# Two-layer decoder trunk on 8 cores: the first rows and mixer units issued one behind the other, norm rows and fourth feed-forward slot later, background casts placed anew

## What is computed

```python
h = layer_norm(DEEPNORM_ALPHA * h + mix, ln1_g[i], ln1_b[i])
h = layer_norm(DEEPNORM_ALPHA * h + sqrelu_mlp(h, mlp_w_up[i], mlp_w_down[i]), ln2_g[i], ln2_b[i])
gate = jax.nn.sigmoid(h @ ple_w_gate[i] + ple_b_gate[i])
h = h + gate * (p[i] @ ple_w_proj[i])
```

## Time and profile before

| | us |
|---|---|
| median of 3 runs | 3253.4 |
| the three runs | 3247.75, 3253.4, 3253.92 |
| the profiled execution, its own time | 3248.94 |
| its span, first to last instruction, slowest core (core 5) | 3247.1 |
| spans of the 8 cores | 3213.3 to 3247.1 |
| PE busy on core 5 | 3081.9 (95%) |
| PE idle on core 5 | 165.2 |

### The profile page before, as it was taken

The page is one execution under the profiler, slowest core; times in us unless marked ns, Lnnn a source line. Parts: engine busy times, 40 slices in busy tenths (PEclk is TensorE's granted clock), DMA queues, the critical chain, the costliest instruction groups (busy, mean ns, idle before and its releaser), DMA issues.

```text
span 3247.1 us, 46641 instructions; the slowest of 8 cores (3213.3 to 3247.1 us)
## 1 busy us (share of the span) xinstructions
PE 3081.9 (95%) x15776; PEld 1446.8 (45%) x15776; DVE 1475.4 (45%) x2583; ACT 1658.3 (51%) x2936; POOL 881.8 (27%) x551
## 2 busy tenths in 40 slices
PE   5989986899999999999999999999999999999998
PEld 2444443444444444444444444444444444444443
DVE  3460163625354555446443354556424455445614
ACT  3476044654556455544555545555564645655452
POOL 0240051314133242424213142232312224142402
PEclk9999998999999999999999999999999999999999
DMA  8749959578986465563635544463644644344441
GB/s 201 166 109 180 173 166 216 171 169 199 258 208 210 152 195 184 161 228 143 221 126 192 205 143 166 143 185 111 207 177 148 199 152 178 130 147 158 143 172 65
DMA packets 84760, 556.65 MB, mean 171 GB/s; under 512 B 9680, under 2 KB 9936, under 8 KB 27600
## 3 DMA queue, kind: packets, MB, share of 16 engines
q1 hardware_dynamic: 74304, 485.31, 42.7%
q0 software_dynamic: 10224, 68.36, 14.8%
HBM read 564.83 MB, written 85.46 MB: 200 GB/s over the span
## 4 chain that ended last, share of the span: by engine, by line
PE 82%; DMA 7%; DVE 6%; issue 3%; ACT 2%; SPq 0%; DVEq 0%; ACTq 0%; POOLq 0%
PE ps L725 31%; PE ps L1134 24%; PE ps L732 13%; PE ps L1167 6%; DMA mring<-ws 3%; PE ps L1067 2%; DMA xT<-xs 1%; PE ps L1176 1%; PE ps L763 1%; PE ps L1047 1%; DVE ar L751 1%; DVE h L787 1%; DMA h<-x 1%; DMA sring<-wsb 1%; PE ps L1027 1%
## 5 line engine op out<-in xcount | busy, mean ns | idle before, releaser
L725 PE MATMUL ps<-xT,mring 128*128 128x512 bf16 x4096 | 916.3, 381 | 14.2 <-DVE xT L773 5.7
L1134 PE MATMUL ps<-mring,ar 128*128 128x512 bf16 x4096 | 922.2, 379 | 5.2 <-DMA mring<-ws 3.1
L725 PEld LDWEIGHTS ps<-xT,mring 128*128 128x128 bf16 x4096 | 393.7, 98 | 491.3 <-issue 45.2
L1134 PEld LDWEIGHTS ps<-mring,ar 128*128 128x128 bf16 x4096 | 392.6, 98 | 466.9 <-issue 21.5
L781 POOL TENSOR_TENSOR h<-h,lnr_sb 128x1024 f32<-128x1024 f32 x128 | 306.9, 2401 | 853.2 <-ACT rstd L745 432.4
L732 PE MATMUL ps<-sring,xT 128*128 128x512 bf16 x2048 | 469.0, 386 | 6.7 <-DMA sring<-wsb 5.8
L1119 ACT ACTIVATE tmpa<-ps 128x512 f32<-128x512 f32 x512 | 304.7, 596 | 268.6 <-PE ps L725 266.5
L787 DVE SCALAR_TENSOR_TENSOR h<-h,ps 128x512 f32<-128x512 f32 x256 | 173.8, 681 | 566.5 <-PE ps L1134 512.5
L732 PEld LDWEIGHTS ps<-sring,xT 128*128 128x128 bf16 x2048 | 202.0, 100 | 255.7 <-issue 31.1
L782 POOL TENSOR_TENSOR h<-h,lnr_sb 128x1024 f32<-128x1024 f32 x128 | 305.0, 2389 | 12.7 <-POOL h L781 0.4
L1120 ACT ACTIVATE ar<-tmpa 128x512 bf16<-128x512 f32 x456 | 287.2, 630 | 40.8 <-ACT tmpa L1119 1.5
(11 more groups left out here) (139 smaller groups left out, 2750.5 us busy)
## 6 DMA issues: line engine op xcount, KB each, us to landing
mring<-wsb SPq DMA_DIRECT2D x224, 1024.0 KB, 5.7
sring<-wsb SPq DMA_DIRECT2D x116, 1024.0 KB, 6.1
lnr_sb<-lnr SPq DMA_DIRECT2D x32, 1024.0 KB, 5.9
wsb<-ws POOLq DMA_DIRECT2D x23, 1024.0 KB, 17.5
h<-x SPq DMA_DIRECT2D x32, 512.0 KB, 9.1
mring<-ws POOLq DMA_DIRECT2D x16, 1024.0 KB, 20.8
wsb<-mring SPq DMA_DIRECT2D x16, 1024.0 KB, 20.2
y<-h SPq DMA_DIRECT2D x32, 512.0 KB, 6.3
```

Of the source, the lines that this page charges most:

```text
L725: ins = h.matmul(ps[b.i][:], lhsT=wt[:, (m * 8 + kc) * 128:(m * 8 + kc + 1) * 128], rhs=xT[c][:, kc, :], start=(kc == 0), stop=(kc == 7))
L1134: ins = h.matmul(ps[b.i][:], lhsT=hid(kk)[:, t * 128:(t + 1) * 128], rhs=wt[:, kc * 512:(kc + 1) * 512], start=(kk == 0), stop=(kk == 31))
```

## The change

Five edits, all in the streams that issue DMAs.

1. The first three mixer casts used to be issued at once. Now cast 0 waits for the landing of row tile 1 of group 0, and casts 1 and 2 wait for the landing of cast 0.
2. The rows of group 1 waited for the first mixer cast; now they wait for row tile 3 of group 0.
3. The first load of the norm rows was issued first of all; now it waits for the landing of `sring` load 7 (second output-projection unit).
4. `mring` load 3, the fourth slot, had no wait of its own and was issued by POOL right behind the first three mixer casts (the row at 5.54 us below); now it waits for `sring` load 7, as load 2 did and does.
5. The 23 background casts have new places: before `mring` 4, 6, 8, 10, 12, 14, `sring` 9, 11, 13, 15, 17, `mring` 24 to 29 and 40 to 45; now `mring` 4, 6, 8, 10, 12, 14, 15, `sring` 19, 21, 23, `mring` 23, 25, 27, 29, 31 and 34, 36, ... 48.

```diff
--- before.py
+++ after.py
@@ -595,6 +595,7 @@
         cast_done = set()
 
         loads = {"mring": [], "sring": []}
+        first_rows = []
         bg = [L0_N + i for k in ("q", "up", "gt") for i in range(L1_UNITS[k], L1_UNITS[k] + {"q": 5, "up": 16, "gt": 2}[k])]
 
         def loader(R):
@@ -604,8 +605,8 @@
                 buf, res = R.slot(k)
                 uid = u + (L0_N if layer else 0)
                 also = []
-                if R is RM and k < 3:
-                    at = (2, 6, 7)[k]
+                if R is RM and k < 4:
+                    at = (2, 6, 7, 7)[k]
                     yield Until(lambda at=at: len(loads["sring"]) > at)
                     also = [loads["sring"][at]]
                 if uid in bg:
@@ -613,6 +614,9 @@
                     yield Until(lambda uid=uid: f"wsb{uid}" in S.last_w)
                 if uid not in cast_done:
                     cast_done.add(uid)
+                    if R is RS and k < 3:
+                        yield Until(lambda k=k: len(first_rows) > (1, 7, 7)[k])
+                        also = [first_rows[1]] if k == 0 else [mine[0]]
                     o = O("pool", lambda h, buf=buf, uid=uid: h.dma_start(out=buf[:], in_=ws_d[uid]), [], [res], CAST, dma_key="c" + res, also=also)
                     mine.append(o)
                     yield o
@@ -625,7 +629,7 @@
                     R.loaded = k + 1
 
         def caster():
-            places = [("mring", k) for k in range(4, 16, 2)] + [("sring", k) for k in (9, 11, 13, 15, 17)] + [("mring", k) for k in list(range(24, 30)) + list(range(40, 46))]
+            places = [("mring", k) for k in (4, 6, 8, 10, 12, 14, 15)] + [("sring", k) for k in (19, 21, 23)] + [("mring", k) for k in list(range(23, 32, 2)) + list(range(34, 49, 2))]
             todo = [(at, i, f"wsb{uid}", wsb_d[uid], ws_d[uid]) for i, (uid, at) in enumerate(zip(bg, places))]
             for j in range(2, NJ):
                 g, layer = job_of(j)
@@ -642,6 +646,7 @@
 
         def lnr_loader():
             yield Until(lambda: len(loads["sring"]) > 7)
+            first = loads["sring"][7:8]
             for i, e in enumerate(lnseq):
                 yield Until(lambda i=i: state["lnr_used"] >= i)
                 if e < 0 and -1 not in lnseq[:i]:
@@ -651,7 +656,7 @@
                 elif e < 0:
                     yield O("sp", lambda h: h.dma_start(out=lnr[:, 0, :], in_=bos_d[:, :]), ["bos"], ["lnr"], 5e5, dma_key="lnr")
                 else:
-                    yield O("sp", lambda h, e=e: h.dma_start(out=lnr[:].rearrange("p a d -> p (a d)"), in_=lnr_d[e]), [], ["lnr"], 1e6, dma_key="lnr")
+                    yield O("sp", lambda h, e=e: h.dma_start(out=lnr[:].rearrange("p a d -> p (a d)"), in_=lnr_d[e]), [], ["lnr"], 1e6, dma_key="lnr", also=first if i == 0 else ())
                 state["lnr"] = i + 1
 
         def p_loader():
@@ -699,12 +704,16 @@
         def load_h(c, g, layer=0):
             late = ()
             if layer == 0 and g >= 1:
-                at = 0 if g == 1 else first_unit[(g, 0)] + 4
-                yield Until(lambda: len(loads["sring"]) > at)
-                late = loads["sring"][at:at + 1]
+                at = first_unit[(g, 0)] + 4
+                if g > 1:
+                    yield Until(lambda: len(loads["sring"]) > at)
+                late = loads["sring"][at:at + 1] if g > 1 else first_rows[3:4]
             src = hs_d if layer else x_d
             for t in range(NT):
-                yield O("sp", lambda h, t=t: h.dma_start(out=h_tok[c][:, t, :], in_=src[g * G + t * 128:g * G + (t + 1) * 128, :]), [f"hs{g}_{t}"] if layer else [], hn(c, t), 5e5, dma_key=f"h{c}_{t}", also=late)
+                o = O("sp", lambda h, t=t: h.dma_start(out=h_tok[c][:, t, :], in_=src[g * G + t * 128:g * G + (t + 1) * 128, :]), [f"hs{g}_{t}"] if layer else [], hn(c, t), 5e5, dma_key=f"h{c}_{t}", also=late)
+                if len(first_rows) < 8:
+                    first_rows.append(o)
+                yield o
             h_named.add((g, layer))
 
         def spill(c, g):
```

## The result

| | before | after |
|---|---|---|
| median of 6 runs, us | 3251.56 | 3237.09 |
| ratio after to before, 95% interval | | 0.9962 (0.995 to 0.9973) |
| span of the slowest core in the profiled execution, us | 3247.1 | 3234.7 |
| mean span of the 8 cores, us | 3228.8 | 3220.8 |

Faster by 12 us by the ratio and 14 by the medians, where 25 were forecast; the time lies in the range, 11 us above the number.

A forecast was written before the change was run, and what follows sets the result against it. PE, busy 95% of the span, was taken as the bound, plus its 165 us of idle time. Gains 22 + 3 + 5 - 5 = 25 us off 3248.9 gave 3224, stated as 3226; range 3206 to 3246.

The forecast's parts named there:

- edits 1 to 4, to A: Start to the first up matmul: it comes at about 165.5 us, before at 187.44; a gain of 22, bounds 12 and 28.
- 5 (a): Stretch from 225 to 445 us: a background cast moved from its front gains 3 us, bounds 0 and 6.
- 5 (b): Job 2's projections: three casts have left, so write-out and unit come earlier; gain 5 us, bounds -5 and 14.
- 5 (c): Job 3's feed-forward, 780 to 960 us: eight or so casts where six were; loss of 5 us, bounds 0 and -15.
- behind D2: The last two thirds of the program stay as they are and move as a whole.
- the waits between 800 and 1000 us: Sign of a wrong forecast: waits between 800 and 1000 us of more than 15 us.
- The start: Group 0's rows land at 10.5 to 11 us in place of 33.3, v near 22; q and k begin at 41.
- If that cover goes, POOL's products of job 0 are late, not PE: Norm rows land at about 128 us, hidden by 11 us; without that cover POOL's job 0 products are late, not PE.
- The DMA engines are the bound from 225 to 445: Rival, 225 to 445 us: the DMA engines bound it and the start's 22 us are waited away; 3246 us, chance 0.10.
- POOL's queue in job 3: Rival: eight casts from `mring` 34 to 48 each hold POOL's queue for a landing, 46 us; 3265 us, chance 0.04.
- More is freed in job 2: Rival: all waits of 509 to 563 us go, 16.5 us and 2 of slow matmuls; 3212 us, chance 0.07.
- Group 1's rows come too late: Rival at the start: group 1's rows land at 30 us, k and the rest slip up to 8; 3234 us, chance 0.07.

The follow-up runs named there:

- e1: The kernel after with the background casts back at their places of before, the start as changed; ratio to before 0.993.
- e2: The kernel before with only the new places of the background casts; ratio to before 1.004.
- e5: The kernel after with the data of the casts at `mring` 34, 36 and 38 cast behind `sring` load 18, engine orders held; ratio to before 0.992.
- e6: e1 with three casts of the same size into a spare tensor nobody reads added behind `mring` loads 34, 36 and 38; ratio to before 0.9993.
- e8: The kernel after with the norm rows issued without waiting for `sring` load 7, other engines' order kept; ratio to before 0.9979.
- e4: The kernel after with the data of the casts at `mring` 34, 36 and 38 cast behind those at 25, 27 and 29, orders held; ratio to before 0.9996.
- e11: The kernel after with the first mixer cast (v) no longer waiting for row tile 1 of group 0; ratio to before 1.0004.

## Why the prediction was right in sign and wrong in size

| term of the sum | forecast | mean of cores | slowest core |
|---|---|---|---|
| edits 1 to 4, to A | +22 | +18.5 | +16.6 |
| 5 (a), A to B | +3 | +0.1 | +2.4 |
| 5 (b), B to C | +5 | +4.7 | +3.3 |
| 5 (c), C to D2 | -5 | -14.8 | -14.5 |
| behind D2 | 0 | -0.5 | +4.6 |
| sum | 25 | 8.0 | 12.4 |

(The slowest core is core 5 before and core 3 after.)

**The step that failed is 5 (c)**, "I take a loss of 5, bounds 0 and -15". Its direction and lower bound were right, its size was 14.8. With the runs: edits 1 to 4 alone are worth 23 us (e1), near the 22 of the sum; edit 5 was put at 3 + 5 - 5 = +3 and measured -10 (e1 to after) and -13 (e2). One of the prediction's own signs of being wrong came true as well: on core 3 the waits between 800 and 1000 us are 15.5 us (8.6 and 2.3 for transfers, 2.5 and 2.2 for ACT), over its 15. The working set 15 us more of DMA work against 23 us of room in 180 us. But room is no average. In before, core 5, the chain write-out, reload, projection takes 29 us, from 832 to 861, and in these the engines stood at 0.99, with nothing to give; the room of the 180 us lay elsewhere (0.61 from 780 to 809). Before's page and trace had the sign, though I did not read it: the only DMA that this projection waits for is the reload, three times in the span, and one of the three is in this place.

```profile
L725 PE MATMUL ps<-xT,sring 128*128 128x512 bf16 x1152 | 257.5, 384 | 7.6 <-DMA xT<-xs 7.6
```

```profile
861.01 9.19 PE L725 MATMUL ps<-xT,sring 128*128 128x512 bf16 x34 [2.34 <-DMA xT<-xs]
```

(The other two are 0.8 us at 1210 and 4.4 at 1405.) A wait that exists is a chain without slack on that core, and what was put on the engines beside it lengthened it: write-out and reload together took 26.3 us in the mean of before and 41.6 in after, 15.3 more, close to the whole loss. The forecast had priced the average of the stretch and not this chain. The runs show that it is the three casts' traffic and not the order: moved away it gives 11.3 us back (e5), added to e1 it costs 22.5 (e6, with the waits for ACT that come with it).

**The start**: the rows landed at 13.8, not at 10.5 to 11, since four tiles of 0.5 MB took 12 us from 1.5 on where their 6.9 us of work had been the basis. The steps behind are right: 3.6 us to the gate, v at 23.3 (22), q and k at 42.8 (41), the first r unit at 89 (88). Then the second output-projection unit landed at 128.5, not 119, and the norm rows at 152, not 128; POOL waited 22.67 us for them. "If that cover goes, POOL's products of job 0 are late, not PE" held: PE has no wait for them before A, and e8 shows that issuing them first costs 5.5 us more. The four edits together are worth 18.5 us at A; undone one at a time they cost 4.3 (norm rows), 6.7 (fourth slot), 10.9 and 13.5 (the two halves of edit 1). These add up to 35: the edits lean on each other, and each undone alone gives back a good part of the whole. Edit 2 was not undone by itself.

**5 (a)** was too high. PE's waits for `mring<-ws` between 200 and 440 us fell from 5.8 to 3.2 us on the slowest core, but over all cores A to B is 247 to 249 us in every kernel above, whatever the places. What sets the waits that are left there was not tried. **5 (b)** was right in size, though 1.5 of the 4.7 us come without edit 5 (B to C is 266.0 in e1): from the gate of job 2 to its recurrence 57.4 us became 50.2, with 54.8 in e1. The wait of 5.84 us for the DVE product is 0.94 now.

**Rivals.** "The DMA engines are the bound from 225 to 445" is out: B comes 18.6 us earlier. "POOL's queue in job 3" is out for the kernel after, whose PE waits from 820 to 860 for transfers alone (what sets its two waits near 970 was not tried); e4 shows a cast holding POOL for 23.5 us. "More is freed in job 2" is out: B to C gained 4.7 us, not 18. Of "Group 1's rows come too late" the premise came true, the last tile landed at 29.5 us in the mean (30), but PE needs these rows only behind its first v unit, at 33, and waits for them on one core alone, 1.3 us.

## What to carry to other kernels

Background traffic is placed by the chains it lies beside, not by the share of busy DMA time in a long stretch: look first for the transfers that PE already waits for, even by 2 us, and keep everything else from being in flight beside them and close ahead of them. Three casts moved into a hole of the new trace (DMA share 0.26 on core 4, 0.53 on core 3) won 14 us, as much as the whole change had; the same three moved 70 to 100 us earlier, beside others, cost 11 (e4). At this kernel's start, where PE waits for the first bytes, issuing transfers one behind the other in the order of their use was worth more than overlap: rows that had to share with casts came at about 30% of their rate.

## What the runs showed of the hardware

**One core of each pair is slower.** In the profile after, the odd cores end 23 to 28 us behind their even neighbours:

```profile
core 0: 3209.7 us, clock 0.985
core 1: 3232.4 us, clock 0.983
core 2: 3207.1 us, clock 0.986
core 3: 3234.7 us, clock 0.983
```

In all 6 executions of after, each of the pairs 0/1, 2/3, 4/5 and 6/7 has one core 8 to 33 us behind the other, and which one changes from one execution to the next; the profiles of before and of e1 to e11 show the same, with gaps of 5 to 36 us. In the profile after, the mean gap of the four pairs grows by 4.7 us up to A, 4.4 from A to B, 9.5 from B to C, by nothing from C to D2 (where the DMA share of the window above is 1.03), and by 5.9 behind it; what opens it is not shown. The metric is the slowest core, so it always reads the slow side of some pair. The Trainium skill (HBM Reference, Specifications (TRN2)) says that the two cores of a pair share one memory domain; no run here isolates that as the cause.

**Rows beside casts.** Tiles of 0.52 MB on SP's queue came every 7.4 us beside casts and every 2.2 us with none beside them for most of the way (7.07 to 13.78 above), about 30% of the rate. ACT's casts in before, core 5:

```profile
10.98 1.04 ACT L737 CAST ar<-h 128x1024 bf16<-128x1024 f32 x1 [5.53 <-DMA h<-x]
17.49 1.04 ACT L737 CAST ar<-h 128x1024 bf16<-128x1024 f32 x1 [5.46 <-DMA h<-x]
25.28 1.04 ACT L737 CAST ar<-h 128x1024 bf16<-128x1024 f32 x1 [6.75 <-DMA h<-x]
```

The fourth is in the earlier trace rows.
